# A two-block transformer kernel on one core: order of the first mixer's ScalarE work, router and norm sums between output products, filler products, a narrower double norm, HGRN2's sigmoid on ScalarE

## The reference, cut to what matters

```
y = x * rsqrt(mean(x*x) + EPS) * g                       # every norm
x = x + concat([y_a, y_b]) @ w_out ; x = x + hier_moe(rms_norm(x, ffn_norm_g), ...)
x = rms_norm(x, final_norm_g) ; hn = rms_norm_2(x, norm_mix_g_2[0])     # the double norm
log_f = logaddexp(log(lb), log1p(-lb) + log_sigmoid(f))  # HGRN2, f = hn @ w_f
k = (1 - lb) * sigmoid(-f)
o = gated_chunkwise(silu(q) * DK**-0.5, k, i, log_f)     # needs the running sums of log_f
```

## Time and profile before

| | us |
|---|---|
| median of the runs | 2238.21 |
| the profiled execution | 2239.99 |
| its span | 2238.20 |
| TensorE busy | 2015.3 |
| TensorE weight loads | 1275.5 |
| VectorE busy | 615.8 |
| ScalarE busy | 489.3 |
| GpSimd busy | 225.5 |

### The profile page before, as it was taken

One profiled execution on the slowest core, in us unless ns is written; L12 is line 12 of the kernel. 1 busy time (PEld: TensorE's weight loads), 2 busy tenths in 40 slices (PEclk: granted clock), 3 DMA queues, 4 the chain that ended last, 5 costly groups with the idle time before them and its releaser, 6 DMA issues. The chain is left out here.

```text
span 2238.2 us, 38630 instructions
## 1 busy us (share of the span) xinstructions
PE 2015.3 (90%) x16935; PEld 1275.5 (57%) x16935; DVE 615.8 (28%) x1034; ACT 489.3 (22%) x661; POOL 225.5 (10%) x95
## 2 busy tenths in 40 slices
PE   6889787878787898999989898999999999999998
PEld 6788544434443788899979883443343433343334
DVE  4663311111111752554477532000001010000002
ACT  3521111111112542433444411000000000000001
POOL 3530000000000551000155100000000000000000
PEclk8999688888888999999989998999999999999999
DMA  7321399999999531356633325999999999999993
GB/s 275 114 113 37 136 425 424 425 423 425 422 424 417 193 113 57 95 188 192 222 133 111 154 113 185 378 393 418 419 418 405 392 395 419 418 419 419 419 418 126
DMA packets 134763, 653.05 MB, mean 292 GB/s; under 512 B 9824, under 2 KB 32480, under 8 KB 89440
## 3 DMA queue, kind: packets, MB, share of 16 engines
q1 hardware_dynamic: 134624, 650.95, 73.1%
HBM read 649.86 MB, written 1.05 MB: 291 GB/s over the span
## 5 line engine op out<-in xcount | busy, mean ns | idle before, releaser
L1852 PE MATMUL psum<-ring,arena 128*32 128x384 f32 (+1 forms) x3584 | 368.4, 542 | 2.7 <-DMA ring<-in_moe_w_up 1.5
L587 POOL TENSOR_TENSOR ring_r<-ring,ring_r 128x1024 fp32r<-128x1024 f32 x86 | 213.6, 2501 | 991.9 <-ACT ring_r L577 970.3
L524 PE MATMUL psum<-ring_r 128*128 128x256 f32 x944 | 267.8, 284 | 0.0
L1852 PEld LDWEIGHTS psum<-ring,arena 128*32 128x32 f32 x3584 | 114.2, 110 | 221.4 <-issue 214.2
L1914 PE MATMUL psum<-ring,arena 128*32 128x512 f32 x1600 | 199.3, 600 | 4.9 <-DMA ring<-in_moe_w_down 4.9
L522 PE MATMUL psum<-ring_r 128*128 128x256 f32 x608 | 178.2, 293 | 14.9 <-POOL ring_r L587 14.9
L524 PEld LDWEIGHTS psum<-ring_r 128*128 128x128 f32 x944 | 181.8, 193 | 0.0
L523 PE MATMUL psum<-ring_r 128*128 128x256 f32 x608 | 174.1, 286 | 0.0
L2054 DVE TENSOR_TENSOR arena<-arena,psum 128x512 f32<-128x512 f32 (+1 forms) x42 | 23.7, 616 | 506.2 <-PE psum L1858 359.5
L1609 PE MATMUL psum<-ring,arena 128*32 128x512 f32 x1024 | 141.6, 704 | 19.2 <-DMA ring<-in_w_up 19.2
L1631 PE MATMUL psum<-arena 64*128 64x256 f32 x272 | 101.4, 547 | 45.7 <-ACT arena L1691 45.5
(11 more groups left out here) (408 smaller groups left out, 2766.2 us busy)
## 6 DMA issues: line engine op xcount, KB each, us to landing
ring<-in_w_gate SPq DMA_DIRECT2D x64, 1024.0 KB, 15.6
ring<-in_w_down SPq DMA_DIRECT2D x32, 2048.0 KB, 21.0
ring<-in_w_up SPq DMA_DIRECT2D x64, 1024.0 KB, 19.7
ring<-in_moe_w_gate SPq DMA_DIRECT2D x64, 1024.0 KB, 20.0
ring<-in_moe_w_down SPq DMA_DIRECT2D x64, 1024.0 KB, 18.5
ring<-in_moe_w_up SPq DMA_DIRECT2D x48, 1024.0 KB, 17.3
ring<-in_moe_w_gate SPq DMA_DIRECT2D x64, 768.0 KB, 18.8
ring<-in_moe_w_up SPq DMA_DIRECT2D x48, 768.0 KB, 17.3
```

Of the source, the lines that this page charges most:

```text
L524: return nc.tensor.matmul(out, al, bh, start=False, stop=stop, **kw)
L587: eng.tensor_tensor(lo[:, :, c], w[:, :, c], w_hi[:, :, c].bitcast(F32), ALU.subtract)\
L1852: mm = nc.tensor.matmul(bank(b0 + j)[n * MORE:(n + 1) * MORE, 0:Q], z_Xg[:, x:x + MORE], w[:, (2 * h + j) * Q:(2 * h + j + 1) * Q], start= ...
```

## The change

- **Mixer 1.** ScalarE makes RSTD and the high tokens first and q's weights after; the gates come behind the keeping of q; a_h (with the rounding of a_c) is kept ahead of the convolutions' SiLU. VectorE makes q's two low quarters behind the tokens.
- **Between output blocks.** `finish` calls `following(r)` after the second, third and fourth pair: the router's or the next norm's quarters 0 to 2. Quarter 3 follows alone.
- **Fillers.** `keep_warm(b, n)` issues n products of ones by ones, 128x128, into a bank that nobody reads.
- **Double norm.** The squares are the weights of products with 8 columns (four of ones, four of final_g squared), so a token's sums stand in its row; Ln, Exp and products work on 16 columns, and two products with the unit matrix lay the factors out again in banks 5 and 4.
- **HGRN2.** 1/(1+u) is Exp(-Ln(1+u)) on ScalarE, the affine step is the scale and bias of the Ln behind it, in parts of two heads.
- **Second expert stage.** `share(i + 1)` stands behind `hidden`, the last norm's quarters 0 to 2 between the spreads.

```diff
+        def keep_warm(b, n):
+            for _ in range(n):
+                nc.tensor.matmul(bank(b)[:, 0:P], ones[:, :], ones[:, :], start=True, stop=True)
+        def norm_tensor(pe, st, r):
+            pe.wait_ge(*S[st].at(f"n_sq{r}"))
+            for k in (2 * r, 2 * r + 1):
                 mm = nc.tensor.matmul(bank(7)[:, 0:T], ones[:, :], SQ[:, k * T:(k + 1) * T],
                                       start=(k == 0), stop=(k == KC - 1))
...
-            def finish(self, ready):
+            def finish(self, ready, following):
...
                     if b % 2:
                         mm.then_inc(*E[self.st].step())
+                        if b > 1:
+                            following(b // 2 - 1)
...
         def mixer1_tensor(pe):
-            norm_tensor(pe, st)
+            keep_warm(5, 8)
+            for r in range(4):
+                norm_tensor(pe, st, r)
+            keep_warm(5, 26)
             project_first(pe, st, "one", "q")
...
-            out.finish(v.at("y"))
+            out.finish(v.at("y"), lambda r: route_quarter(pe, M1, r))
...
         def mixer1_scalar(act):
-            weights_hi_of(act, st, "one", "q", range(2))
             act.wait_ge(*e.at("n_sum"))
...
-            tokens_hi(act, st, more_weights)
+            tokens_hi(act, st)
+            weights_hi_of(act, st, "one", "q", range(4))
...
-            act.wait_ge(*v.at("logits"))
+            def gates():
+                act.wait_ge(*v.at("logits"))
...
             for n, w in enumerate("qkv"):
                 keep(w, lambda half: m1_convin[:, 4 * n + 2 * half:4 * n + 2 * half + 2, 3:3 + T])
-            round_next(act, st, "one", PROJ1, "a_h", 0)
+                if n == 0:
+                    gates()
+            keep("a_h", lambda half: m1_ahx[:, 2 * half:2 * half + 2, 2:2 + T])
             act.wait_ge(*v.at("conv2"))
...
-            keep("a_h", lambda half: m1_ahx[:, 2 * half:2 * half + 2, 2:2 + T], rounded=1)
...
+        WARM = {"moe1": (34, 4), "moe2": (16, 4)}
+            route_quarter(pe, m, 3)
+            keep_warm(2, WARM[m.name][0])
             pe.wait_ge(*v.at("chosen"))
...
+            keep_warm(2, WARM[m.name][1])
...
         def mixer2_tensor(pe):
+            for r in range(4):
+                pe.wait_ge(*s.at(f"n_sq{r}"))
+                for k in (2 * r, 2 * r + 1):
+                    for t in range(NT):
+                        at = k * T + t * P
+                        mm = nc.tensor.matmul(bank(7)[:, 8 * t:8 * t + 8], SQ[:, at:at + P],
+                                              n_weights[:, 8 * k:8 * k + 8], start=(k == 0 and t == 0),
+            keep_warm(6, 7)
+            for n, (steps_of, name, cols_) in enumerate(((V, "n_both", n_second), (S, "n_first", n_first))):
+                pe.wait_ge(*steps_of[st].at(name))
+                for t in range(NT):
+                    mm = nc.tensor.matmul(bank(5 - n)[:, t * P:(t + 1) * P],
+                                          cols_[:, 8 * t:8 * t + 1].to_broadcast([P, P]), eye,
+            keep_warm(6, 6)
...
             proj("bv", rows_=True)
+            pe.wait_ge(*v.at("x"))
             gated_tensor_round(pe, GLA, 0)
...
         def ffn_tensor(pe):
-            norm_tensor(pe, st)
+            norm_tensor(pe, st, 3)
+            keep_warm(6, 9)
...
         def hgrn_tensor(pe):
-            norm_tensor(pe, st, [V["ffn"].at("x")])
+            keep_warm(3, 8)
+            pe.wait_ge(*V["ffn"].at("x"))
+            for r in range(4):
+                norm_tensor(pe, st, r)
+            keep_warm(6, 10)
...
+            def sigmoid(half, part):
+                act.wait_ge(*v.at(f"h{half}u{part}"))
+                nc.scalar.activation(out, x.k[:, part * 512:(part + 1) * 512], ACT.Ln, bias=1.0)
+                nc.scalar.activation(out, out, ACT.Exp, scale=-1.0).then_inc(*s.step())
+                for h in (2 * part, 2 * part + 1):
+                    nc.scalar.activation(x.g[:, hs], x.y[:, hs], ACT.Ln, bias=c_lb[:, n:n + 1],
+                                         scale=c_omlb[:, n:n + 1]).then_inc(*s.step())
...
-                do(nc.vector.tensor_scalar(x.g, x.k, 1.0, None, ALU.add))
-                do(nc.vector.reciprocal(g, g))
-                    nc.vector.tensor_scalar(x.g[:, hs], x.g[:, hs], c_omlb[:, n:n + 1], c_lb[:, n:n + 1],
...
             def item(i):
-                share(i)
...
                 for b in range(2):
                     hidden(i, b)
+                share(i + 1)
                 if is_large(i):
                     keep_y(i)
```

More of the change, by code:

```diff
@@ L2604, in do @@
                 dve.wait_ge(*v.last())
+            first, second, sums = (x[:, 0:16].rearrange("p (t n) -> p t n", n=8) for x in (n_first, n_second, bank(7)))
             dve.wait_ge(*s.at("n_first2"))
-            nc.vector.tensor_tensor(n_second, n_second, bank(7)[:, T:2 * T], ALU.mult).then_inc(*v.step())
+            nc.vector.tensor_tensor(second[:, :, 0:4], second[:, :, 0:4], sums[:, :, 4:8], ALU.mult)\
+                .then_inc(*v.step())
             v.name("n_second")
             dve.wait_ge(*s.at("n_second"))
-            nc.vector.tensor_tensor(RSTD, n_first, n_second, ALU.mult).then_inc(*v.step())
-            dve.wait_ge(*v.last())
+            nc.vector.tensor_tensor(second[:, :, 0:4], first[:, :, 0:4], second[:, :, 0:4], ALU.mult)\
+                .then_inc(*v.step())
+            v.name("n_both")
+            dve.wait_ge(*e.at("n_rstd"))
             for r in range(4):
-                nc.vector.tensor_tensor(quarter(hT, r), quarter(hT, r), RSTD.unsqueeze(1).to_broadcast([P, 2, T]),
+                nc.vector.tensor_tensor(quarter(hT, r), quarter(hT, r), bank(5)[:, 0:T].unsqueeze(1).to_broadcast([P, 2, T]),
                                         ALU.mult).then_inc(*v.step())
@@ L2934, in hgrn_scalar @@
             s.name("lbexp")
+            act.wait_ge(*v.at("bounds"))
             def keep(half, what, out, **kw):
                 keep_banks(act, st, f"h{what}{half}", PROJ3, B3, out, **kw)
-            def log_decay(half):
-                act.wait_ge(*v.at(f"h{half}f"))
-                nc.scalar.activation(HG[half].g, HG[half].g, ACT.Ln).then_inc(*s.step())
-                s.name(f"h{half}ln")
-            keep(0, "f", halves(HG[0].k), func=ACT.Exp, scale=-1.0)
+            def sigmoid(half, part):
+                x = HG[half]
+                out = x.y[:, part * 512:(part + 1) * 512]
+                act.wait_ge(*v.at(f"h{half}u{part}"))
+                nc.scalar.activation(out, x.k[:, part * 512:(part + 1) * 512], ACT.Ln, bias=1.0).then_inc(*s.step())
+                act.wait_ge(*s.last())
+                nc.scalar.activation(out, out, ACT.Exp, scale=-1.0).then_inc(*s.step())
+                s.name(f"h{half}sig{part}")
+                act.wait_ge(*s.last())
+                for h in (2 * part, 2 * part + 1):
+                    hs = slice(h * T, (h + 1) * T)
+                    n = half * H4 + h
+                    nc.scalar.activation(x.g[:, hs], x.y[:, hs], ACT.Ln, bias=c_lb[:, n:n + 1],
+                                         scale=c_omlb[:, n:n + 1]).then_inc(*s.step())
+                s.name(f"h{half}ln{part}")
+            for part in range(2):
+                keep(0, "f", halves(HG[0].k), func=ACT.Exp, scale=-1.0, parts=(part,))
+                sigmoid(0, part)
             keep(0, "q", halves(HG[0].q), func=ACT.Silu)
             act.preload_act_table_set(EXP_LN)
-            log_decay(0)
             keep(0, "i", halves(HG[0].v))
@@ L3048, in second @@
                 v.name(f"h{half}ready")
-            forget_start(0)
-            forget_reciprocal(0, 0, H4)
-            forget_end(0)
+            for part in range(2):
+                forget_start(0, part)
+            for part in range(2):
+                forget_end(0, part)
             second(0)
```

203 lines of the change are left out of this document (102 added, 101 removed).

## The result

The changed kernel takes 2207.7 us, the kernel before 2238.4 us on the same chip: 30.7 us less by these medians, 34.7 by the ratio of 0.9845 (95% interval 0.9832 to 0.9858). Forecast were 2190 us, 48 less, in a range of 2178 to 2208. So the direction was right, the time lies at the edge of the range, and about a third of the expected gain is missing. One of its five executions took 2449 us at a mean clock of 0.78 against 0.95 and is left out of the ratio.

What follows compares the result with a forecast made beforehand. TensorE, busy 90% of the span, was taken as the bound, leaving its idle and low-clock time to win. Terms -15.5 -5 -4 +1.2 -1.9 -17 -3.7 -1.9 sum to -47.8, giving a median of 2190 us, range 2178 to 2208.

Steps and rivals of the forecast that it cites:

- the signs that the prediction named: Profile marks that would confirm it: first product near 18.7, k near 34.4, L827 near 105, first router's clock above 0.8.
- Mixer 1: First mixer: both TensorE waits (4.63 and 10.22 us) go, L827 comes at 104.8 to 105.5 instead of 121.03: -15.5 us.
- it ends at about 77.7, the normalisation at 87.5, and a_b's products at 104.8: Mixer 1's convolution chain: starts 6 us sooner and ends sooner still, as GpSimd's weight parts come sooner too.
- HGRN2: HGRN mixer: scans end at 1154 to 1158.6, before TensorE wants them at 1160.2, so its waits go: -17 us.
- R2: Rival in HGRN: VectorE's minimums and products each wait for a GpSimd operation, gain 6 not 17, 2201 us; chance 0.15.
- The routers and the clock: Both routers: earlier sums, cheaper counts, and in the first a faster spread, through higher clock: -5 and -3.7 us.
- the 2.1 of the first spread: First router: at high clock the spread saves about 3.6 us, of which the forecast counted 2.1.
- The clock terms: Gains from fillers holding TensorE's clock in mixer 1, routers and other places, 15.6 us together.
- Double norm, FFN norm, HGRN norm: The norm stages: -4 us for the double norm, +1.2 for the FFN norm, -1.9 for the HGRN norm.
- The end: Second expert stage's end: share(i+1) moved earlier gives 1.4, final sums between the spreads 0.5: -1.9 us.
- the prediction's estimate with it: Mixer 1's term if the skill page's drain of about 1380 ns per function-set switch held: -12.8 us instead of -15.5.
- the prediction's reading: HGRN, under R2: operations with two SBUF inputs share GpSimd's interface, so scans and products suffer, the minimum not.

Runs made afterwards that it cites:

- the second set: The changed kernel executed again, unchanged, to get a profile at the usual clock: median 2208.81 us beside 2239.71 before, ratio 0.9865.
- the kernels with short and with moved parts: Changed kernel with GpSimd's weight parts of mixer 1 and HGRN2 cut to 64 elements (2665 us), or low parts given to VectorE (hg0's 2200.42, all 2191.84).
- twice the fillers: The changed kernel with the routers' first filler groups doubled, 34 to 68 and 16 to 32: 2214.93 us, ratio 0.9883.
- mixer 1's order alone: The kernel before with only mixer 1's new order on ScalarE, VectorE and GpSimd, without fillers: 2229.81 us, ratio 0.9953.
- hg0's low parts on VectorE: The changed kernel with hg0's four low weight parts made by VectorE instead of GpSimd, without the double norm's seven fillers: 2200.42 us, ratio 0.9826.
- all low parts: The changed kernel with hg0's and mixer 1's low parts behind q on VectorE, without the double norm's seven fillers: 2191.84 us, ratio 0.9783.

## Why the prediction was right, and where it was not

That the range holds is in part luck: 2207.7 lies 0.3 us inside it, the 2208.81 of the second set 0.8 outside. Of the signs that the prediction named, the first product (18.3), k (34.9) and a_c without a wait came; the product of L827 near 105 (108.6), the first router's clock above 0.8 (0.69), the mixer 2 projection under 5 us behind the sums (6.3) and no wait above 2 us before the scores (5.73) did not. Two steps miss 5.3 and 7.1 us.

**Mixer 1, the largest miss but one: -10.2 for -15.5.** The two waits, their causes and their end came as told. What failed is the step "it ends at about 77.7, the normalisation at 87.5, and a_b's products at 104.8". The chain ended at 81.2, the sums started at 89.1 and ended at 95.5, and L834 came at 108.6. I had seen the alternation of VectorE and GpSimd, and gave the earlier start of GpSimd's parts as a reason for a sooner end. It is none, for the parts moved along with the convolutions. The chain starts 6.0 sooner, at 37.7, and keeps its length, 43.5 us against 43.8: ten of its 48 operations take the long time beside GpSimd, where twelve did before, and a wait of 4.02 for v is new. Before the change GpSimd had ended at 78.7, ahead of the third convolution; now seven of its parts lie beside it. The wait of 5.38 that is left then costs its clock as well, 2.8 us in the sums, for which the forecast had no term. Behind the sums a_b's and z's parts meet the normalisation, steps of 2.4, 3.4 and 4.5 us that take 1.2, 1.2 and 1.3 alone, and a new wait of 2.03 stands before L848: from L834, which comes 12.5 sooner than before, to y another 2.3 are lost. The measured price of the sharing in mixer 1 is 9.5 to 9.6 us, the clock that its waits cost included; part of it was there before the change.

**HGRN2: -9.9 for -17.** The scans end at 1139.7, ahead of TensorE's 1144.3, as forecast. The failed step is that the waits of 7.8 and 5.3 both go with nothing late behind. R2 named the mechanism and gave it 0.15, but priced it at 15.6 on the steps before the scans, which took 6.3 (3.8 for four products, 1.2 and 1.3 for the minimums). It struck behind the scans, in six operations of rounds 0 and 1 that take 2.8 to 3.4 us each. Before the change the same operations had GpSimd idle beside them (its parts end at 1166.7 and start again at 1176.2, a pause in which TensorE's wait of 7.8 ends), and now they have not. The stall that went had kept the two engines apart in the next stretch. That the causes are these, the kernels with short and with moved parts show; that TensorE's wait held the copies, and with them GpSimd's parts, is read from the order of times alone. The prediction also had against R2 that the operations of before took their plain time beside GpSimd. Two of them did not: the plus-one (L3020) took 2.78 us where the minimum of the same size took 1.49, and the second product (L3032) 2.62 where the last two took 0.47. "What is late next" had to be asked of the operations behind the scans too.

**The routers and the clock: -2.8 and -3.1 for -5 and -3.7.** The terms for the last quarter and the counts came; the 2.1 of the first spread did not: it still takes 7.16, the same as in the earlier trace rows. The clock falls at 234.4, ahead of the gather, and with twice the fillers it falls at 252.0, in the idle time between gather and spread; either way the spread runs at 0.50. The clock terms as a whole were put at 15.6; leaving the fillers out costs 6.7 (9.2 between the profiles).

**Double norm, FFN norm, HGRN norm** were right within 0.6, the double norm by other parts than I had: 1.4 at the first product (not 3.4, for the seven fillers and a column sum of 5.9 us), and 2.0 in the projection (not 0.6).

**The end, -4.7 for -1.9.** The number is not the forecast's. What follows the last expert product, where share(i+1) and the sums between the spreads work, takes 17.4 us instead of 19.0: 1.6 less. At the stage's start 2.1 are lost. The second router's gather is now at high clock, but VectorE's steps beside it still take their time, so TensorE waits 4.31 us instead of 1.19, the clock falls in this wait, and the first expert products run at 0.50:

```profile
1329.30 3.64 PE L1870 MATMUL psum<-ring,arena 128*32 128x512 f32 x16 [4.31 <-DVE arena L2115]
```

In the kernel before the same sixteen take 1.92. So two thirds of the second router's 3.1 are given back. The other 5.1 to 5.2 us are clock inside the stage: the kernel before has 6.8 us at 0.50 from 1575.1 (3.3 us) and again from 2073.5, where the changed kernel has only 3.4 us (1.8). The first of these stands at the same place in the kernel with mixer 1's order alone (from 1569.5), and 540 us into the stage in three others (hg0's low parts on VectorE, all low parts, twice the fillers); the other profiles have it at neither place. No run tells what brings it. Without it the profiles' 34.0 us would be nearer to the 30.7 and 30.9 between the medians.

On the switch of function set: the changed kernel's load again takes 1.28 us and the next activation starts 0.01 behind it (86.62, 87.91), no drain of 1.38. The Trainium skill ("ScalarE: Activation LUTs", What ACT_TABLE_LOAD costs) states such a drain, and the prediction's estimate with it was -12.8. The measured -10.2 is a still smaller gain, but not for that reason.

## What to carry to other kernels

When two engines share the way to SBUF, count their operations together: take from the engine that is free only if its slower operations don't lie beside those of the engine on the path. Where a wait goes, look one round further than the step that had it: what the wait had kept apart from the other engine now meets it. A filler product is free only as far as the pause it stands in; read the pause in the trace at the clock that holds there (seven cost 3.3 us in a pause of 1.8). And before a sum of steps is compared with one profile, look how far the profiles of unchanged stretches differ (2 us in mixer 1, 5 in the second experts here).

## What the runs showed of the hardware

- VectorE and GpSimd alternated, one operation each, in the slow stretches above, where both work on SBUF: a VectorE operation of 0.47 us took 2.6, one of 0.69 took 2.8 to 2.9. A run of VectorE operations that had the turn kept it once: GpSimd's operation then took 7.33 instead of 2.4. An operation with a PSUM input (L1177, at 103.60) kept its 1.22 us in the middle of a GpSimd operation (102.45 to 105.84). Before the change the reciprocal (6.55) had three GpSimd operations beside it that took no longer than alone (2.42 to 2.60), so not every operation takes part. What gives an engine the turn, no run tells.
- An operation with one SBUF tensor could be held too: L1136 of the third convolution takes 2.0 us in the mean (8.01 for four) against 0.28 (1.13 for four) alone. The Trainium skill ("VectorE: DVE Perf Modes", Two Vector instructions with no wait between them) names two SBUF inputs or a 2-port mode for the interface shared with GpSimd; the prediction left the second condition out. The rows don't tell which mode this operation ran in, but the prediction's reading, that the minimum would not suffer, fell: in the second half two minimums of 512 columns took 2.2 us each, in the first half 1.2 and 1.3.
- In the kernel with twice the router's fillers the granted clock was 0.50 for the first 3.4 us of the 68 fillers (from 224.7) and 1.00 from 228.1 to 252.0, through the other fillers (to 241.6), the counts and the gather. In the changed kernel it fell at 234.4, 4.2 us behind the end of 34 fillers, after a wait of 1.8 us, the count products and four more fillers, and the gather ran at 0.50 again.
